# Three product stages made one, and the two scan directions added inside the scan

## The reference, cut to what matters

```python
# scan over chunks; s is the state, one scan forward and one backward
v_new = u_n - w_n @ s
o     = qd_n @ s + qk_n @ v_new
s     = s * exp(gl_n) + kd_n.T @ v_new

# end of the layer; h is x normalised, scaled and shifted
za, ga, gb = h @ w_za, h @ w_ga, h @ w_gb
ya = rmsnorm(o_f + reverse(o_b)) * gdn_norm_w * silu(za)
y  = sigmoid(ga) * (ya @ w_proj_a) + sigmoid(gb) * (yb @ w_proj_b)
x  = x + gate * (y @ w_out)
```

## Time and profile before

| | |
|---|---|
| median of 3 runs | 3046.15 us (3042.67 to 3047.25) |
| the profiled execution | 3047.45 us |
| its span, first to last instruction | 3045.6 us |
| PE busy | 2877.6 us |
| DVE, ACT, POOL busy | 1551.8, 1144.5, 247.9 us |
| mean granted PE clock | 0.976 of full speed |
| the scan | 539.8 to about 600 us of the span |
| gates, merge, output | 603.1 to 734.9, 738.3 to 784.9, 791.2 to 839.0 us |

### The profile page before, as it was taken

The page is one execution under the profiler, slowest core; times in us unless marked ns, Lnnn a source line. Parts: engine busy times, 40 slices in busy tenths (PEclk is TensorE's granted clock), DMA queues, the critical chain, the costliest instruction groups (busy, mean ns, idle before and its releaser), DMA issues.

```text
span 3045.6 us, 43045 instructions
## 1 busy us (share of the span) xinstructions
PE 2877.6 (94%) x17460; PEld 2416.3 (79%) x17460; DVE 1551.8 (51%) x2616; ACT 1144.5 (38%) x1863; POOL 247.9 (8%) x276
## 2 busy tenths in 40 slices
PE   5999989799999999999999999899999999999997
PEld 2887879767778888877888888788888778888886
DVE  5734466453454433765554435644435855644346
ACT  3333544242243322456433324533324554433234
POOL 0000055500000000110100000000000201000000
PEclk8999999999999999999999999999999999999998
DMA  6112000022223222310132232233233201232321
GB/s 227 63 64 82 1 9 3 12 73 87 79 97 97 97 97 83 120 61 29 63 111 97 97 104 77 71 109 97 97 104 109 94 29 42 90 97 97 104 91 56
DMA packets 69780, 244.95 MB, mean 80 GB/s; under 512 B 8464, under 2 KB 10640, under 8 KB 68944
## 3 DMA queue, kind: packets, MB, share of 16 engines
q1 hardware_dynamic: 69584, 242.21, 24.0%
HBM read 234.70 MB, written 3.15 MB: 78 GB/s over the span
## 4 chain that ended last, share of the span: by engine, by line
PE 66%; DVE 3%; ACT 2%; issue 1%; DVEq 0%; ACTq 0%
PE pair L228 20%; PE pair L229 19%; PE pair L230 19%; PE pair L2585 2%; PE pair L2614 2%; PE pair L352 2%; PE pair L2624 1%; ACT w_hi_at L182 1%; DVE rstd_at L468 1%; DVE work_at L303 0%; DVE w_lo_at L190 0%; PE pair L486 0%; DVE residual L309 0%; DVE h_lo_at L314 0%; PE pair L483 0%
## 5 line engine op out<-in xcount | busy, mean ns | idle before, releaser
L228 PE MATMUL pair<-h_hi_at,w_hi_at 128*128 128x512 f32 (+1 forms) x2048 | 780.0, 381 | 35.9 <-DVE h_lo_at L314 31.6
L229 PE MATMUL pair<-h_lo_at,w_hi_at 128*128 128x512 f32 (+1 forms) x2048 | 758.5, 370 | 0.0
L230 PE MATMUL pair<-h_hi_at,w_lo_at 128*128 128x512 f32 (+1 forms) x2048 | 758.4, 370 | 0.0
L190 DVE TENSOR_TENSOR w_lo_at<-w_raw,w_hi_at 128x1024 fp32r<-128x1024 f32 x348 | 439.4, 1263 | 430.6 <-ACT w_hi_at L182 430.3
L182 ACT ACTIVATE w_hi_at<-w_raw 128x1024 fp32r<-128x1024 f32 x348 | 364.8, 1052 | 523.1 <-PE pair L230 511.7
L228 PEld LDWEIGHTS pair<-h_hi_at,w_hi_at 128*128 128x128 f32 x2048 | 388.1, 190 | 113.0 <-DVE h_lo_at L314 37.9
L229 PEld LDWEIGHTS pair<-h_lo_at,w_hi_at 128*128 128x128 f32 x2048 | 388.4, 190 | 66.8 <-issue 0.5
L230 PEld LDWEIGHTS pair<-h_hi_at,w_lo_at 128*128 128x128 f32 x2048 | 388.2, 190 | 65.0
L2347 DVE TENSOR_TENSOR work_at<-pair,rstd_at 128x512 f32<-128x512 f32 (+1 forms) x184 | 122.2, 667 | 363.2 <-PE pair L230 363.1
L228 PE MATMUL pair<-a_hi_at,w_hi_at 128*128 128x512 f32 (+1 forms) x792 | 290.1, 366 | 0.0
L229 PE MATMUL pair<-a_lo_at,w_hi_at 128*128 128x512 f32 (+1 forms) x792 | 289.4, 365 | 0.0
(11 more groups left out here) (418 smaller groups left out, 4100.1 us busy)
## 6 DMA issues: line engine op xcount, KB each, us to landing
w_raw<-in_weights SPq DMA_DIRECT2D x431, 512.0 KB, 3.5
residual<-in_x SPq DMA_DIRECT2D x1, 2048.0 KB, 11.8
cos_sin_at<-rope_table SPq DMA_DIRECT2D x2, 1024.0 KB, 4.9
by_sin_at<-delta_at SPq DMA_DIRECT2D x32, 64.0 KB, 2.0
by_sin_at<-kd_at SPq DMA_DIRECT2D x32, 64.0 KB, 2.0
out<-residual SPq DMA_DIRECT2D x16, 128.0 KB, 1.7
q_wide<-in_ctx SPq DMA_DIRECT2D x1, 1024.0 KB, 12.9
rope_table<-zb SPq DMA_DIRECT2D x1, 1024.0 KB, 4.9
```

The lines of the kernel that those rows point to most:

```text
L190: eng.tensor_tensor(self.w_lo[:, g % self.split].rearrange("p k n -> p (k n)"), self.w_raw[:, g % RAW], self.w_hi[:, g % self.split].rearr ...
L228: pe.matmul(out, sh, mh, start=start, stop=False)
L229: pe.matmul(out, sh, ml, start=False, stop=False)
L230: return pe.matmul(out, sl, mh, start=False, stop=stop)
```

## The change

One function `closing` takes the place of `gates_product`, `merge` and the output's `project_tiles`: 36 tiles in one stage, each engine with one list for all of them. Its buffers are all placed together; `part_a`, `part_b`, `y`, `y_hi` and `y_lo` take the place of buffers that the gates no longer need. The scaled parts of x read the spread rstd straight from its PSUM bank. The ones-matmuls come behind tiles 3 and 6. Merge tile u and output tile v take bank pairs in the order 3, 1, 2, 0. The weights of the next part are split during the last tiles of the part before.

In the scan, the last step makes no `k_rest`, faded state or new state. In steps 4 and 5 the direction that comes second to a chunk is added by DVE, from its PSUM bank, to the other direction's output in `q_dec`, straight into `o`. Functions without a caller are dropped.

```diff
 # delta_scan, PE
-                        pe.wait_ge(prepared[d], 3 * s + 2)
...
-                        last.then_inc(s_summed[d], 1)
+                        if s < LAST:
+                            pe.wait_ge(prepared[d], 3 * s + 2)
...
+                            last.then_inc(s_summed[d], 1)
                         if c < XCH:
-                            if s > 2:
+                            if 2 < s <= ALONE:
                                 pe.wait_ge(out_ready, 2 * (s - 3) + d + 1)
+                            if s > ALONE:
+                                pe.wait_ge(out_added, 2 * (s - ALONE - 1) + d + 1)
 # delta_scan, DVE, behind the two states of a step
+                        if s == LAST:
+                            continue
...
+                    if s < ALONE:
+                        continue
+                    for d in range(2):
+                        c = order[d][s]
+                        dve.wait_ge(out_summed[d], s - 1)
+                        dve.wait_ge(out_ready, XCH)
+                        dve.tensor_tensor(o[:, :, c * P:(c + 1) * P], heads(bank[6 + d][:, :]), heads(q_dec[:, 1 - d, c]),
+                                          ALU.add).then_inc(out_added, 1)
 # closing, PE
+                spread_columns(kit, pe, rstd_columns, XCH, 7).then_inc(spread, 1)
+                for t in range(GATES):
...
+                    if t == 3:
+                        sums(0)
+                    if t == 6:
+                        sums(2)
+                for u in range(KD):
+                    if u == 0:
+                        pe.wait_ge(rooted, HEADS)
+                    elif u < 4:
+                        pe.wait_ge(drained, 14 + 2 * u)
+                    else:
+                        pe.wait_ge(y_drained, u - 3)
+                    pe.wait_ge(kit.w_split, g1 + u + 1)
...
+                for v in range(OUT):
+                    if v < 4:
+                        pe.wait_ge(y_drained, v + 5)
+                    else:
+                        pe.wait_ge(out_drained, v - 3)
+                    pe.wait_ge(kit.w_split, g2 + v + 1)
+                    for k in range(KD):
+                        if v == 0:
+                            pe.wait_ge(y_rested, k + 1)
+                        last = matmul3(pe, merge_banks(v)[0], kit.w_tile(g2 + v, k), (y_hi[:, k], y_lo[:, k]), k == 0, k == KD - 1)
 # closing, ACT, behind the gates
+                for u in range(KD):
+                    kit.w_make_hi(act, g1 + u + 2)
+                    act.wait_ge(y_ready, u + 1)
+                    act.activation(y_hi[:, u], y[:, u % 2], ACT.Copy).then_inc(y_rounded, 1)
 # closing, DVE
+                dve.wait_ge(spread, 1)
+                normed.dve_part(dve, 0, 3, lambda: kit.w_make_lo(dve, g0))
                 kit.w_make_lo(dve, g0 + 1)
-                dve.wait_ge(spread, 1)
-                dve.tensor_copy(rstd_x[:, :], kit.banks[1][:, :]).then_inc(rows_ready, 1)
...
+                normed.dve_part(dve, 3)
+                for t in range(GATES):
+                    kit.w_make_lo(dve, g0 + t + 2)
+                    if t in (5, 6, 8, 9):
+                        norm(t - 5 if t < 7 else t - 6)
...
+                for u in range(KD - 1):
+                    kit.w_make_lo(dve, g1 + u + 2)
+                    merge(u)
+                merge(KD - 1)
+                kit.w_make_lo(dve, g2 + 1)
```

More of the change, by code:

```diff
@@ L241, in __init__, with dve_part @@
         self.scaled, self.rounded, self.rested = sem("scaled"), sem("rounded"), sem("rested")
-    def dve_part(self, dve):
+    def dve_part(self, dve, first=0, last=None, behind_first=None):
+        last = self.tiles if last is None else last
         def rest(t):
@@ L251, in rest @@
                                          ALU.subtract).then_inc(self.rested, 1)
-        for t in range(self.tiles):
+        for t in range(first, last):
             if t >= 2:
@@ L260, in dve_part, with act_part @@
                                          ALU.mult).then_inc(self.scaled, 1)
-            if t >= 1:
+            if t == first and behind_first:
+                behind_first()
+            if t > first:
                 rest(t - 1)
-        rest(self.tiles - 1)
-    def act_part(self, act):
-        for t in range(self.tiles):
+        rest(last - 1)
+    def act_part(self, act, first=0, last=None):
+        last = self.tiles if last is None else last
+        for t in range(first, last):
             act.wait_ge(self.scaled, t + 1)
@@ L576, in _ @@
                 s.dve(dve)
[L579 to L605, removed]
 def beside_gemm(eng, make, g0, k_tiles, tiles, body, beside_first=None, beside_second=None):
@@ L1002, in _ @@
                 beside_gemm(dve, kit.w_make_lo, g0, GK, tiles, body, of_x.dve_part, of_ctx.dve_part)
[L1005 to L1042, removed]
 def heads_and_gates(kit, h, raw, tokens, heads, tables, loads, gate_cols, g):
@@ L1894, in _ @@
                         pe.wait_ge(v_ready[d], s + 1)
[L1895 to L1899 removed]
+                        if s < LAST:
+                            pe.wait_ge(prepared[d], 3 * s + 2)
+                            for h in range(HEADS):
+                                hs = slice(h * P, (h + 1) * P)
+                                last = pe.matmul(bank[4 + d][:, hs], k_rest[:, d, hs], v_new[:, d, hs], start=True, stop=True)
+                            last.then_inc(s_summed[d], 1)
                         if c < XCH:
[L1901 removed]
+                            if 2 < s <= ALONE:
                                 pe.wait_ge(out_ready, 2 * (s - 3) + d + 1)
+                            if s > ALONE:
+                                pe.wait_ge(out_added, 2 * (s - ALONE - 1) + d + 1)
                             for h in range(HEADS):
@@ L1967, in _ @@
+            rstd_bank = kit.banks[7]
+            normed = normed_h(kit, sem, h_buf, kit.residual, SEQ, 0, rstd_bank, h_hi, h_lo, 0)
+            sum_bank = lambda i: kit.banks[RING + i % 2][:, :]
+            merge_banks = lambda u: [kit.banks[2 * PAIRS[u % 4] + which] for which in range(2)]
             @block.sync
             def _(sp):
-                fetch_ahead(kit, sp, g0, tiles)
+                fetch_ahead(kit, sp, g0, GATES + KD + OUT)
             @block.tensor
@@ L1978, in sums @@
                         pe.matmul(sum_bank(i), kit.square("ones"), sq[:, i], start=True, stop=True).then_inc(summed, 1)
[L1980 to L1983, removed]
+                spread_columns(kit, pe, rstd_columns, XCH, 7).then_inc(spread, 1)
+                for t in range(GATES):
+                    if t >= RING:
+                        pe.wait_ge(drained, t - RING + 1)
                     pe.wait_ge(kit.w_split, g0 + t + 1)
@@ new lines, in _ @@
+                for u in range(KD - 1):
[3 more added lines that the diff above has]
+                kit.w_make_lo(dve, g2 + 1)
+                for v in range(OUT):
+                    if v + 2 < OUT:
+                        kit.w_make_lo(dve, g2 + v + 2)
+                    dve.wait_ge(kit.w_used, g2 + v + 1)
+                    dve.scalar_tensor_tensor(kit.residual[:, v], merge_banks(v)[0], kit.gate[:, v:v + 1], kit.residual[:, v],
+                                             ALU.mult, ALU.add).then_inc(out_drained, 1)
@@ L2176, in first_block @@
                 delta_inverse(kit, q, k, cols, levels, inverse, attend, q_dec)
[L2177 to L2200 removed]
+            delta_scan(kit, k, k_tok, v_tok, cols, inverse, attend, q_dec, o)
+        closing(kit, o, yb, rstd_columns)
 def normed_h(kit, sem, buf, src, width, who, rstd, h_hi, h_lo, at):
@@ L2207, in normed_h @@
                   lambda t: kit.shift[:, t, who:who + 1])
-def split(kit, src, tiles, hi, lo):
-    with stage(kit) as (block, sem):
-        rounded = sem("rounded")
-        @block.scalar
-        def _(act):
-            for t in range(tiles):
-                act.activation(hi(t), src(t), ACT.Copy).then_inc(rounded, 1)
-        @block.vector
-        def _(dve):
-            for t in range(tiles):
-                dve.wait_ge(rounded, t + 1)
-                dve.tensor_tensor(lo(t), src(t), hi(t).bitcast(F32), ALU.subtract)
 class Ffn:
```

179 lines of the change are left out of this document (70 added, 109 removed).

## The result

| | before | after |
|---|---|---|
| median of 4 runs each, side by side | 3046.03 us (3042.67 to 3047.25) | 3021.64 us (3016.54 to 3023.56) |
| ratio, 95% interval | | 0.9921, 0.9909 to 0.9933 |
| the profiled execution, its span | 3047.45, 3045.6 us | 3022.48, 3020.7 us |
| mean granted PE clock | 0.976 | 0.980 |

24.4 us less, where 3022.0 and 23.8 less were forecast. The busy line of the page after, beside the earlier trace rows: PE's busy time fell by 8.4 us. The 16 `k_rest` matmuls that are no longer made are 1.8 of it (two groups of 0.89); most of the rest are products that ran slowly before.

What follows compares the result with a forecast made beforehand. TensorE (PE), busy 94% of the span, was taken as the bound. Terms 4.5 + 0 + 4.8 + 5.2 + 9.3 = 23.8 us took the profiled 3047.45 to 3023.65, median 3022 us; range 3018.5 to 3028.

Steps and rivals of the forecast that it cites:

- scan's end: Last scan step to the gates' spread: fewer matmuls, one addition and one barrier let the new stage begin 4.5 us earlier.
- head of the gates: Start of the gates' stage: rstd copy saved, weight splits reordered; no change taken, between 0.5 us gain and 0.8 loss.
- square sums: Second ones-matmul pair moved behind the seventh tile: 3.3 us idle and 1.5 us slow matmuls gone, gain 4.8 us.
- joint of gates and merge: Last gates matmul to second merge tile: excess of 5.2 us, 3.4 idle and the rest slow products, all gone.
- joint of merge and output: Last merge product into the output's first tile: excess of 9.26 us, 6.45 standing still and 2.8 slow, taken whole.
- rival 2: Gates' head: new holes keep the clock down into the first full tiles, 2.8 us back, 3025 us; 14%.
- rival 1: Output's start: last y_lo or late second weight still holds PE up, 5.1 us back, 3027 us; 8%.
- Signs: What the changed profile should show, among it no PE idle from first gates tile to last output tile, busy time nearly unchanged.
- Rivals 3 to 5: Order changes but time stays, some 3043, 2%; splits late on every tile, 3058, 2%; clock falls under unbroken work, 1%.

Runs made afterwards that it cites:

- e1: Kernel before with only the scan's part of the change, everything from the gates on as before; 3037.24 us beside 3047.41 for the kernel before.
- e2: Changed kernel with the square sums' ones-matmuls back behind tiles 3 and 4, all four roots behind tile 4; 3028.26 us.
- e4: Changed kernel, still one stage without barrier, but the first two merge weights are split only after the gates are done; 3025.78 us.
- e3: Changed kernel, but the first output tile waits for all eight split parts of y at once instead of part by part; 3024.58 us.
- e6: Changed kernel with the head's old order, both weight splits ahead of the parts of h, rstd still read from PSUM; 3022.38 us.
- e9: Changed kernel with a barrier between gates and merge, first merge weight split ahead of it, the second behind it; 3020.51 us.
- e5: Changed kernel cut in two stages by a barrier between gates and merge, first two merge weights split ahead of it; 3028.93 us.
- e11: The changed kernel itself, unedited, timed again in later rounds; 3020.07 us, ratio 0.9915 to the kernel before.

## Why the prediction was right, step by step

| step | forecast | in the profiles | what undoing it cost |
|---|---|---|---|
| scan's end | 4.5 | 4.53 | (alone: 4.54, e1) |
| head of the gates | 0, from -0.8 to +0.5 | 0.46 | |
| square sums | 4.8 | 4.97 | 6.2 (e2) |
| joint of gates and merge | 5.2 | 5.20 | 4.7 (e4) |
| joint of merge and output | 9.26 | 9.26 | 5.5 (e3: the wait for y only) |
| sum | 23.8 | 24.4 | |

- **Scan's end.** The `k_rest` groups, 1.78, are gone, and one addition of 0.69 and one barrier of 0.40 take the place of a copy, two barriers and four additions. The two additions ahead of the last step's `scan_r` ended at 590.30, and `scan_r` then still waited 0.20 for PE: the cover held. The step ahead is 10.59 us from `scan_r` to `scan_r` in both profiles.
- **Head.** The price zero was between two effects that e6 parts: 0.76 for the copy, where I had counted 0.68, and 0.30 lost by the new order. That all 0.46 came has luck in it: the clock was back in time in this profile, and in others was not (rival 2 below). The last part of h ended 613.06 + 1.63 - 599.16 = 15.53 us after the stage's start, at the early end of the 15.5 to 16.8 forecast.
- **Square sums.** Now an excess of 633.67 - 626.75 - 5.60 = 1.32 and 0.39 for the first pair, 1.72 with the second: 3.43 in all, the sums' own work. By the same count the three tiles before had 1.32, 6.62 and 0.46, 8.40 together. I had priced the slow part by the pair alone, 1.5; products behind it were slow too. DVE's narrow place held: the `w_lo` that ended at 678.89 was needed at 680.58, 1.7 ahead where I had counted 1.3.
- **Gates and merge.** Whole, and by the step that I named, the splits during the last gates tiles (e4). With these early splits, being one stage is worth 1.2 (e9).
- **Merge and output.** Whole. The prediction calls 6.45 of the 9.26 standing still; the wait itself is 6.28, and the other 0.17 is the end of the last product, 0.40 long where the pace is 0.23. The wait for y is worth 5.5 (e3); no run undoes the rest, 3.8 for the late weights and the barrier, by itself, so it is read from the timelines alone. The seventh and eighth `y_lo` ended 0.2 and 3.6 us after merge's last product (forecast 0.2 and 3.7), the second output weight 4.7 after it, 0.75 ahead of the tile that uses it. The margin of 0.7 on which rival 1 rested was real and stayed.
- **Signs.** All came as named but one: PE's busy time was to be nearly unchanged and fell by 8.4 us. The prediction's own terms hold most of that: 1.5 + 1.6 + 2.8 = 5.9 of slow products and 1.8 of `k_rest` matmuls.
- **Rivals.** Rival 1 did not happen; brought about in e3, it cost 5.5, near its price. Rivals 3 to 5 fell with the timeline. Rival 2, the cold head, fell due in part. In five of the eight profiles with the new head (e2, e3, e5, e9, e11) the clock came up and fell again 12.1 to 12.6 us after the spread's start. In three of them it was back before the second gates tile, which began 0.2 to 0.3 us later than in the change. In e5 and e9 that tile began with the clock down, and together with the longer first tile this cost (17.43 - 16.39) + 0.9 = 1.9 us, less than the 2.8 forecast. The Trainium skill (TensorE: Matmul & The Clock Gate, Part 1: The HAM clock gate) calls the moment at which the gate opens run-variable; these eight profiles agree, with first tiles of 6.27 to 7.32 us excess from the same code.

That the sum came within 0.4 us of the median has luck in it: upstream scatter alone moves a run by several us.

## What to carry over

Price a joint by the excess over the pace of the undisturbed stream, not by the idle time: the slow products behind a pause of 2.8 us or more were worth 1.5 to 2.9 us here. Then ask what the first tile behind the joint waits for. With the barrier kept, splitting its weight ahead of the barrier was worth 4.0 us (the kernel before against e9), and taking the barrier out after that 1.2; taking out the barrier alone would have been worth 0.5 (the kernel before against e4). A preparation that must wait for the last tile cost 3.3 more ahead of the barrier than behind it (e5 against e9). Where a true dependence remains, let the consumer take its input part by part: its first tile then hides the producer's tail.

## What was not expected of the hardware

- Whether a pause costs more than its own length is not settled by its length alone. Behind 1.00 us of standing still (e9) the granted clock stayed at 1.00 and only 0.2 was lost beyond the pause. Behind 2.80, 2.94 and 3.7 us (e5, e4, e3) it went to 0.50 when PE was already back at work, and the first tile took another 1.60 to 1.62 us. In between lies a pause of 1.58 us that every kernel here has in the last stage, behind a dense stream of products. In six of the thirteen profiles (e1, e2, e4, e6, e9, e11) the clock fell behind it, in seven it stayed; behind a pause of the same length some 1100 us later it stayed in all thirteen. The first place in the kernel before, where the clock stayed, in the timeline of PE and in a stretch:

```profile
1877.30 0.39 PE L228 MATMUL pair<-h_hi_at,w_hi_at 128*128 128x256 f32 x1 [1.58 <-DVE w_lo_at L190]
```

```profile
1879.00:1880.00 1.00, 1.00 (x11) 1.00 (x10) 1.00 (x3) 0.96 (x3) 0.00 (x0) 1.00 0.73 295
```

and in e6, where it fell:

```profile
1853.74 0.39 PE L228 MATMUL pair<-h_hi_at,w_hi_at 128*128 128x256 f32 x1 [1.58 <-DVE w_lo_at L190]
```

```profile
1855.00:1856.00 1.00, 1.00 (x7) 1.00 (x6) 1.00 (x4) 1.00 (x4) 0.00 (x0) 0.50 0.78 283
```

- The slow part varies between executions of the same code: behind the 6.28 us pause of the old output joint the first tile's excess was 2.81 us in the profile of before and 1.51 in e1.
- In the head after the change the clock came back to 1.00 during 608 to 609 while PE stood still, and the matmuls from 609.53 on ran at full pace.
